# Stored high and low halves of output, down and projection weights in a one-core hybrid encoder layer

## What is computed

```python
mod = silu(c) @ w_ada + b_ada                  # shift, scale, gate; twice
h = rmsnorm(x, g_pre_mix) * (1 + sc1) + sh1
xa, xb, xc = split(h @ w_in)                   # 256 + 768 + 1152 columns
ya = pool_mixer(xa); yb = conformer_conv(xb); yc = short_conv(xc)
x = x + gt1 * rmsnorm(concat(ya, yb, yc) @ w_out, g_post_mix)
h = rmsnorm(x, g_pre_ffn) * (1 + sc2) + sh2
f = (silu(h @ w_gate) * (h @ w_up)) @ w_down
x = x + gt2 * rmsnorm(f, g_post_ffn)
```

## Time and profile before

| | |
|---|---|
| median of 3 runs | 2259.43 us (2258.07 to 2260.43) |
| span of the profiled execution | 2256.9 us, 2.5 us below the median |
| TensorE busy | 2241.4 us, 99% |
| VectorE busy | 1348.1 us, 60% |
| ScalarE busy | 1003.7 us, 44% |
| DMA | 368.98 MB, mean 163 GB/s |
| weight splits | 531 on ScalarE, 560.8 us; 531 on VectorE, 646.6 us |

### The profile page before, as it was taken

One profiled execution on the slowest core, in us unless ns is written; L12 is line 12 of the kernel. 1 busy time (PEld: TensorE's weight loads), 2 busy tenths in 40 slices (PEclk: granted clock), 3 DMA queues, 4 the chain that ended last, 5 costly groups with the idle time before them and its releaser, 6 DMA issues.

```text
span 2256.9 us, 29984 instructions
## 1 busy us (share of the span) xinstructions
PE 2241.4 (99%) x12270; PEld 2069.5 (92%) x12270; DVE 1348.1 (60%) x1967; ACT 1003.7 (44%) x1419; POOL 38.2 (2%) x83
## 2 busy tenths in 40 slices
PE   9999999999999999999999999999999999999998
PEld 6779998979999988999898899989899998899987
DVE  3779966698444677744467854357784535443343
ACT  3455465454354534344544435254443425432332
POOL 0000000000000000000000000000000000000000
PEclk9999999999999999999999999999999999999999
DMA  9864654554443533544353363435335444444332
GB/s 375 310 218 168 239 202 140 177 169 166 170 151 129 181 127 122 186 150 154 126 185 123 123 213 122 157 123 187 122 127 181 123 131 154 154 150 159 123 129 94
DMA packets 103046, 368.98 MB, mean 163 GB/s; under 512 B 12631, under 2 KB 14807, under 8 KB 102396
## 3 DMA queue, kind: packets, MB, share of 16 engines
q1 hardware_dynamic: 102910, 367.06, 47.8%
HBM read 348.02 MB, written 19.00 MB: 163 GB/s over the span
## 4 chain that ended last, share of the span: by engine, by line
PE 89%; DVE 4%; DMA 1%; ACT 1%; issue 0%; SPq 0%; DVEq 0%; ACTq 0%
PE ps L650 89%; DVE wlo L1377 2%; DVE pr L1528 1%; DMA raw<-in_w_mix 1%; PE ps L720 1%; DVE early L1528 1%; PE ps L680 0%; DVE g_lo L1429 0%; ACT whi L980 0%; DVE h_lo L1422 0%; DMA raw<-in_w_gu 0%; ACT h_f L1048 0%; DVE xt L1446 0%; ACT junk L1003 0%; DVE pr L1550 0%
## 5 line engine op out<-in xcount | busy, mean ns | idle before, releaser
L1377 DVE TENSOR_TENSOR wlo<-raw,whi 128x1024 fp32r<-128x1024 f32 x531 | 646.6, 1222 | 521.9 <-ACT whi L980 520.6
L650 PE MATMUL ps<-h_hi,whi 128*128 128x384 f32 (+1 forms) x2808 | 920.9, 328 | 1.8 <-DVE h_lo L1422 1.0
L980 ACT ACTIVATE whi<-raw 128x1024 fp32r<-128x1024 f32 x531 | 560.8, 1058 | 811.6 <-DMA raw<-in_w_gu 528.7
L650 PE MATMUL ps<-h_hi,wlo 128*128 128x384 f32 (+1 forms) x2808 | 919.3, 327 | 0.0
L650 PE MATMUL ps<-h_lo,whi 128*128 128x384 f32 (+1 forms) x2808 | 919.2, 327 | 0.0
L650 PEld LDWEIGHTS ps<-h_hi,whi 128*128 128x128 f32 x2808 | 528.4, 188 | 7.0 <-issue 4.7
L650 PEld LDWEIGHTS ps<-h_lo,whi 128*128 128x128 f32 x2808 | 528.4, 188 | 0.5
L650 PEld LDWEIGHTS ps<-h_hi,wlo 128*128 128x128 f32 x2808 | 528.4, 188 | 0.0
L650 PE MATMUL ps<-whi,g_hi 128*128 128x512 f32 x748 | 235.1, 395 | 1.7 <-issue 0.9
L650 PE MATMUL ps<-whi,g_lo 128*128 128x512 f32 x748 | 231.1, 390 | 0.0
L650 PE MATMUL ps<-wlo,g_hi 128*128 128x512 f32 x748 | 230.8, 390 | 0.0
(11 more groups left out here) (148 smaller groups left out, 1313.6 us busy)
## 6 DMA issues: line engine op xcount, KB each, us to landing
raw<-in_w_gu SPq DMA_DIRECT2D x264, 512.0 KB, 3.3
raw<-in_w_mix SPq DMA_DIRECT2D x150, 512.0 KB, 3.3
raw<-in_w_dn SPq DMA_DIRECT2D x132, 512.0 KB, 3.3
xr<-in_x_all SPq DMA_DIRECT2D x29, 512.0 KB, 5.9
xr<-x_all SPq DMA_DIRECT2D x17, 512.0 KB, 5.8
pre<-in_w_ada SPq DMA_DIRECT2D x16, 512.0 KB, 10.4
x_all<-xr SPq DMA_DIRECT2D x5, 1536.0 KB, 7.5
xr<-in_w_ada SPq DMA_DIRECT2D x12, 512.0 KB, 7.9
```

The source lines that it names most:

```text
L650: return nc.tensor.matmul(out, lhsT, rhs, start=start, stop=stop, skip_group_check=True)
L980: nc.scalar.activation(whi[:, s, :], raw[:, s, :], ACT.Copy).then_inc(w_hi, 1)
L1377: tt(wlo[:, s, :], raw[:, s, :], whi[:, s, :].bitcast(F32), ALU.subtract).then_inc(w_lo, 1)
```

## The change

Three kinds of weights are kept after they were split: the units of "out" and "dn" of block 1 and of "in" of block 2 (`SPLIT_IN`). `keep_halves` on SP writes whi and wlo of such a unit to a tensor `halves` in device memory, three units behind the load (STORE_LAG); a kept slot is loaded again only when its stores have landed. For all later blocks of the same kind (`from_halves`) two DMAs load the halves straight into whi and wlo, no split is made, and PE waits for the landing. "gu" units, and "in" of blocks 0 to 2 and "out" and "dn" of blocks 0 and 1, are loaded and split as before. The diff in full:

```diff
--- before.py
+++ after.py
@@ -102,13 +102,36 @@
 WARM = (10, 2, 1)
 
 
+SPLIT_IN = {"in": 2, "out": 1, "dn": 1}
+HALVES = NIN + NMIX + NF
+STORE_LAG = 3
+
+
 def whole(n):
     return n < PARTS0 or PARTS1 <= n < NIN
 
 
+def half_row(n):
+
+    kind, _, i = STREAM[n][:3]
+    return {"in": 0, "out": NIN, "dn": NIN + NMIX}[kind] + i
+
+
+def kept(n):
+    return STREAM[n][0] in SPLIT_IN and STREAM[n][1] == SPLIT_IN[STREAM[n][0]]
+
+
+def from_halves(n):
+    return STREAM[n][0] in SPLIT_IN and STREAM[n][1] > SPLIT_IN[STREAM[n][0]]
+
+
+def split_here(n):
+    return not whole(n) and not from_halves(n)
+
+
 def splits(n):
 
-    return sum(not whole(i) for i in range(n + 1))
+    return sum(split_here(i) for i in range(n + 1))
 
 UNIT = {key: n for n, key in enumerate(STREAM)}
 
@@ -227,7 +250,7 @@
 
 def build(nc, x_all, x_cols, c_all, consts, consts_a, cols, gpost, b_ada, w_ada, w_mix, w_pool, w_gu, w_dn,
           st_pool, st_conv, st_sconv, y_all, o_pool_p, o_conv_p, o_sconv_p,
-          o_pool_s, o_conv_s, o_sconv_s, x1_all, gates):
+          o_pool_s, o_conv_s, o_sconv_s, x1_all, gates, halves):
     ctx = ExitStack()
     with ctx:
         def sb(name, shape, dt=F32, scope=ctx, align=ALIGN):
@@ -311,6 +334,7 @@
         four_landed = [sem(f"four_landed{i}") for i in range(len(FOURS))]
         four_used = sem("four_used")
         w_landed = [sem(f"w_landed{i}") for i in range(RING)]
+        halves_stored = [sem(f"halves_stored{i}") for i in range(RING)]
         x_landed = sem("x_landed")
         cols_landed = sem("cols_landed")
         sq_landed = sem("sq_landed")
@@ -379,7 +403,11 @@
         y_v = y_all.rearrange("(n p) d -> p n d", p=P)
 
         def landed(n):
-            return 16 * (n // RING + 1)
+            return sum(32 if from_halves(i) else 16 for i in range(n % RING, n + 1, RING))
+
+        def stored_halves(n):
+
+            return 32 * sum(kept(i) for i in range(n % RING, n + 1, RING))
 
         def four_place(f, i):
 
@@ -473,7 +501,29 @@
                     sp.wait_ge(w_used, n - RING + 1)
                 else:
                     sp.wait_ge(pre_used, group_under(n))
-                sp.dma_start(raw[:, n % RING, :], source(n)).then_inc(w_landed[n % RING], 16)
+                if n >= RING and kept(n - RING):
+                    sp.wait_ge(halves_stored[n % RING], stored_halves(n - RING))
+                if from_halves(n):
+                    i = half_row(n)
+                    if i in (0, NIN, NIN + NMIX) and STREAM[n][1] == SPLIT_IN[STREAM[n][0]] + 1:
+                        wait_halves(n)
+                    sp.dma_start(whi[:, n % RING, :].bitcast(F32), halves[0, i]).then_inc(w_landed[n % RING], 16)
+                    sp.dma_start(wlo[:, n % RING, :].bitcast(F32), halves[1, i]).then_inc(w_landed[n % RING], 16)
+                else:
+                    sp.dma_start(raw[:, n % RING, :], source(n)).then_inc(w_landed[n % RING], 16)
+                if n >= STORE_LAG and kept(n - STORE_LAG):
+                    keep_halves(n - STORE_LAG)
+
+            def keep_halves(n):
+                sp.wait_ge(w_lo, splits(n))
+                sp.dma_start(halves[0, half_row(n)], whi[:, n % RING, :].bitcast(F32)).then_inc(halves_stored[n % RING], 16)
+                sp.dma_start(halves[1, half_row(n)], wlo[:, n % RING, :].bitcast(F32)).then_inc(halves_stored[n % RING], 16)
+
+            def wait_halves(n):
+                for s in range(RING):
+                    kept_ = sum(kept(i) for i in range(s, n - STORE_LAG, RING))
+                    if kept_:
+                        sp.wait_ge(halves_stored[s], 32 * kept_)
 
             def load_x(b):
                 for t in range(NT[b]):
@@ -650,7 +700,10 @@
                 return nc.tensor.matmul(out, lhsT, rhs, start=start, stop=stop, skip_group_check=True)
 
             def wait_split(n):
-                pe.wait_ge(w_lo, splits(n))
+                if from_halves(n):
+                    pe.wait_ge(w_landed[n % RING], landed(n))
+                else:
+                    pe.wait_ge(w_lo, splits(n))
 
             def ada_group(g):
 
@@ -981,7 +1034,7 @@
 
             def ahead(*key):
                 n = UNIT[key] + LEAD
-                if n < TOTAL and not whole(n):
+                if n < TOTAL and split_here(n):
                     high(n)
 
             def x_square(q, t, i=None):
@@ -1918,6 +1971,7 @@
     aps += [nc.dram_tensor(f"out_{k}", s, F32, kind="ExternalOutput").ap() for k, s in outs.items()]
     aps.append(nc.dram_tensor("x1_all", (TILES * P, D), F32, kind="Internal").ap())
     aps.append(nc.dram_tensor("gates", (2, ROWS, D), F32, kind="Internal").ap())
+    aps.append(nc.dram_tensor("halves", (2, HALVES, P, D), F32, kind="Internal").ap())
     build(nc, *aps)
     r = run_bass_kernel_spmd(nc, [{f"in_{k}": v for k, v in ins.items()}], core_ids=[0]).results[0]
 
```

## The result

| | before | after |
|---|---|---|
| median | 2260.26 us (7 runs, 2258.07 to 2260.7) | 2266.63 us (7 runs, 2265.28 to 2268.43) |
| ratio | | 1.0029 (95% interval 1.002 to 1.0039) |
| span of the profiled execution | 2256.9 us | 2265.7 us |

The account below looks back on a forecast made before the run. PE's matmul count was taken as the bound from 516.6 us on. The profiled span of 2256.9 us plus 0.3 us of slip gave 2257.2, and 2.5 us from span to median gave 2259.7 us, range 2257.0 to 2267.0.

Parts of the forecast that it names:

- What bounds the kernel: From 516.6 us the number of matmuls at PE's own pace; VectorE's splits on the path only from 454.8 to 516.6 us.
- the removed work: 171 of 531 units no longer split, 181 us of ScalarE and 209 us of VectorE, all off the path: 0 gained.
- waits of PE after 702 us: Sign of being wrong: PE waiting where units from stored halves are used, a stretch said to wait for nobody.
- SP's queue: Two more issues and one wait for `low` per kept unit, the wait met some 6 us after `low` is done: 0.
- rival (3): SP's order, a store's wait for `low` or a slot's for its stores, holds loads: +4 us, 2264; chance 0.04.
- The rates: DMA engines carry 400 to 420 GB/s against 369 to 385 asked by a kept unit; lower end 343.
- Slices at full share with 345 to 370 GB/s: Sign that the DMA queue is too slow in the kept stages, named beside late loads and PE waiting for `wlo`.
- rival (2): DMA queue too slow in the kept stages, below about 375 GB/s: 2270 us at 343, 2264.5 at 360; chance 0.15.
- The backlog: In "in" of block 2, x1 store and residual loads leave 5.8 us queued at 425 us; loads land after 9.1 us.
- The forgiveness: A load in an "in" stage may land some 11 us after issue; VectorE catches up, slip 0 to 2, 0.3 taken.
- The sum: Span 2256.9 + 0.3 = 2257.2 us, the median 2.5 us above the span: 2259.7 us.
- nothing on the path moves: The forecast case: nothing on the path moves by over 2 us, 2258.5 to 2262 us; chance 0.75 including rival (5).

Follow-up runs that it names:

- c1: The changed kernel with the stores of a unit issued two units behind its load instead of three (STORE_LAG = 2); 2272.12 us, 1.0052 of before.
- a1: The changed kernel with "in" weights neither stored nor loaded as halves, only "out" and "dn"; 2260.65 us, 0.9996 of before.
- a4: The changed kernel with block 1's x1 store and two residual loads moved behind "dn" units 3 and 8 of block 0; 2265.36 us, 1.0015 of before.
- e1: The changed kernel with a3's VectorE pause and "out" and "in" stored one block later ("out" 2, "in" 3); 2264.60 us, 1.0018 of before.
- a3: The changed kernel with VectorE made to wait for GpSimd's ffn-norm rstd before the mixer steps, from block 3's projection on; 2264.80 us, 1.0017 of before.
- b4: The kernel before, no halves stored, with mixer steps moved from block 0's "dn" units to "in" of block 2 and block 1's gate and up; 2257.28 us, 0.9984.
- b5: The changed kernel with the edits of e1 and b4 together; 2259.63 us, 1.0001 of before.
- after_again: The changed kernel measured and traced once more, nothing altered; 2268.77 us, 1.0036 of before.

## Why the prediction was right or wrong

**What bounds the kernel** held. T2 is 1643.41 to 1643.47 us in every kernel with the old steps whose loads and GpSimd adds are undisturbed, with 531 splits or with 360, and no kernel beat it by freeing engines. The value of the removed work was 0, as put. But the text's own sign of being wrong, waits of PE after 702 us, came: two of 1.2 us, behind GpSimd's adds.

**SP's queue** was taken as 0 and is a part of the loss. I looked at one of its two waits, the one for `low`, and found it free (2.3 us in all, on loads that had slack); the other, of a load for the stores of its slot, got half a clause under rival (3). With stores that land after 8.7 to 12.6 us from 418 us on, instead of 6 to 8, it holds the load of "dn" unit 3 for 1.1 us beyond PE. c1 shows how narrow the place between the two waits is.

**The rates** were sized well. Where a backlog stands the engines move 415 to 418 GB/s (420 to 450 us), against 400 to 420 put. Elsewhere they move what is asked: 374 to 391 GB/s from 360 to 420 us, and in the second kept stage

```profile
820.00:830.00 10.00, 10.00 (x45) 8.28 (x45) 7.06 (x11) 4.01 (x6) 0.00 (x0) 1.00 0.99 374
850.00:860.00 10.00, 10.00 (x47) 8.26 (x46) 8.15 (x13) 5.61 (x8) 0.00 (x0) 1.00 0.99 363
```

with 369 asked. Slices at full share with 345 to 370 GB/s had been named as a sign of rival (2), and are none: the landing times there stay at 5.1 to 6.4 us and do not grow. Rival (2) did not happen as told. By the Trainium skill's rule (DMA: Bandwidth & Descriptors, Where 436 GB/s comes from) some 358 GB/s would have been the ceiling; the rows of after at 415 and 418 GB/s contradict it for mixed loads and stores, as the earlier trace rows did for loads. Missed was a place with a higher demand: the first stored units, loaded every 2.9 us (a1).

**The backlog.** The landing of 9.1 us came out near: between 425 and 450 us loads landed after 7.8 to 10.5 us, median 9.5. Its two parts did not, so this is in part luck. A load in the kept stage lands after 5.3 to 6.3 us ahead of the x1 transfers (364 to 414 us) and after 5.5 to 5.9 in a4 without them, not after the 3.3 of a bare load, and the x1 transfers add some 3.8 us to that, not 5.8.

**The forgiveness is the step that failed.** I took 11 us from issue to landing, 7.7 more than a bare load needs, from ScalarE's evacuation two units on; and I let VectorE catch up in some 12 us of which a quarter is idle, 3 us, and kept 0.3 of slip, with 0 to 2 from outside. The load that counts is that of "dn" unit 3, the last one split before VectorE's stretch. It landed 6.5 us late, less than 7.7, and only 2.6 us were forgiven, 1.5 on ScalarE and 1.1 on VectorE: the term is 3.8 us. Behind that split VectorE has three mixer steps, a g_lo and the next split, and from there on no pause at all. In e1 the limit of 11 us is the one that counts; a landing after 11.68 us there, of a load that SP issued late as well, went with 3.6 us.

**GpSimd** stood nowhere in the prediction, and is 3.0 us, nearly half of the result. The 209 us of VectorE's splits were costed as work that disappears. They were also the pauses in which GpSimd's adds went through: 0.20 us for an add when VectorE stands, 8.8 when it runs. The signs were in the trace of before: x_rstd is on ScalarE's way to an evacuation, and VectorE's idle time, put down to `whi`, is what the change takes away. I had asked who waits for the removed operations, and not who lives on the wait in front of them. The Trainium skill (SBUF — State Buffer, SBUF: two separate sides) has the two engines share a port pair that one of them holds for a whole instruction while the other is blocked, among others when VectorE reads two operands from SBUF. The two timelines and a3 agree, with 0.20 against 8.8 us; by the page's wording a wait of one instruction would be looked for, and here it lasted over some sixteen (8.8 us at 0.53 each).

**The sum.** 2259.7 us was the time of the case "nothing on the path moves", and it did not happen; 2266.63 lies in the range, 0.4 us below its upper end, because of rivals (2) and (3), which were to give it by other means: that it lies inside is luck. In the second set of runs the kernel was 8.3 us over before, which would be outside. Also, the change is slower by over 0.2% (1.0029), to which the text gave 0.18. The mechanism of the first part is that of rival (2) and (3) together, at a third of the price of the one and without the condition that was to decide it; that of the second part, GpSimd, is no rival's.

## What to carry to other kernels

Work that is removed from an engine off the critical path also removes the pauses it caused: before counting the gain as zero, look for who used them, GpSimd beside VectorE first. A transfer that lands later is forgiven only as far as the tightest operation that stands behind it in the program of each engine that waits for it, so walk both engines' programs to the end of the stage and into the next (here 2.6 us, where 7.7 had been counted on), and each wait on the issuing queue, the one for a buffer's stores included. Where one engine is the bound for a short stretch, moving its deferrable steps (b4, 3.2 us) is worth more than taking 198 us of work off it elsewhere, which bought nothing.

## What the runs showed of the hardware

- A GpSimd tensor_tensor of 128 x 3 values took 0.20 us beside an idle VectorE and 8.8 to 9.1 us beside an unbroken run of VectorE's scalar_tensor_tensor operations, ending with the run.
- Stores and loads mixed in one queue ran at 415 to 418 GB/s over 20 us, no slower than loads alone at the start.
- A load of 512 KB landed 3.3 us after its issue in before, after 5.3 to 6.3 us between stores of halves at 374 to 391 GB/s, and after up to 10.5 us (e1: 12.2 us) behind a backlog.
- On SP the issue of a 512 KB load takes 0.33 us on an idle queue and up to 1.10 us in after on one that is backed up (at 431.54 us), that of a store 0.43 to 0.50 us in a quiet part of a kept stage and up to 1.46 us (at 423.97 us; e1: 1.32 us at 784.66), so a full queue can also slow the sequencer that feeds it.
- After a wait of PE of 1.9 to 2.8 us the granted clock sometimes fell to the lower level for 3.4 us: after at 458.6 us, a3, e1 and b5 near 328 us, b5 at 801 us; it did not after a wait of 2.1 us in after_again or 2.2 us in b4, nor after 2.7 us in c1. The windows of e1:

```profile
328.00:330.00 2.00, 2.00 (x12) 2.00 (x11) 1.47 (x2) 1.04 (x1) 0.00 (x0) 0.51 0.00 0
330.00:332.00 2.00, 2.00 (x13) 2.00 (x13) 0.30 (x1) 0.00 (x0) 0.00 (x0) 0.64 0.00 0
```

  PE starts 12 and 13 matmuls of 256 columns in 2 us there. The fall in e1 cost 1.7 us ((1 - 0.51) x 2 + (1 - 0.64) x 2). What decides whether it comes was not tried.
